# Down stage: gates fetched in quarters, first down weights one step earlier, lookup splits on DVE, sums by tile

## The reference, cut to what matters

```python
def chunk(xc):
    q = (xc @ w_q).reshape(PEER_CHUNK, PEER_HEADS, 2, PEER_DK_HALF)
    ...
    top_s, top_pos = lax.top_k(cand, PEER_TOPK)
    ids = jnp.take_along_axis(cand_id, top_pos, axis=-1)
    g = jax.nn.softmax(top_s, axis=-1)
    act = jnp.einsum('thkd,td->thk', u[ids], xc)
    w = g * jax.nn.gelu(act, approximate=False)
    return jnp.einsum('thk,thkd->td', w, v[ids])
...
h = h + peer_ffn(rms_norm(h, norm2_g[l]), ...)
```

## Time and profile before

| what | us |
|---|---|
| median of 3 runs | 3421.99 (3420.83 to 3426.84) |
| the profiled execution's own time | 3419.38 |
| its span | 3417.6 |
| PE busy | 3315.4 (97%) |
| DVE busy | 2617.1 (77%) |
| ACT busy | 1554.5 (45%) |
| POOL busy | 1110.6 (32%) |
| mean granted TensorE clock | 0.991 |

### The profile page before, as it was taken

How to read it: one execution, slowest core, us unless ns; L and a number is a source line. 1 busy time by engine, 2 the same in 40 slices (tenths; PEclk the granted TensorE clock), 3 DMA queues, 4 the chain that set the end, 5 groups by cost and what they waited for, 6 DMA issues and landing times.

```text
span 3417.6 us, 55668 instructions
## 1 busy us (share of the span) xinstructions
PE 3315.4 (97%) x19734; PEld 3073.7 (90%) x19734; DVE 2617.1 (77%) x4984; ACT 1554.5 (45%) x2366; POOL 1110.6 (32%) x717
## 2 busy tenths in 40 slices
PE   8999999999999899999999999999999998999998
PEld 7767878999999899999987678889999998999998
DVE  5555439999987788888755544499999877888887
ACT  5554333367773333333345443334677633333333
POOL 0000013433335355545200000143433354555552
PEclk9999999999999999999999999999999999999999
DMA  4113322589999999999621133225899999999996
GB/s 152 63 49 112 136 105 74 186 305 378 381 380 406 398 363 388 390 375 398 262 89 60 50 124 145 93 98 184 320 379 383 381 400 386 376 385 389 368 390 240
DMA packets 231895, 900.59 MB, mean 264 GB/s; under 512 B 21696, under 2 KB 66896, under 8 KB 183872
## 3 DMA queue, kind: packets, MB, share of 16 engines
q1 hardware_dynamic: 116752, 468.22, 36.5%
q0 software_dynamic: 93008, 337.91, 25.6%
q10 hardware_dynamic: 21984, 92.63, 6.8%
HBM read 804.31 MB, written 94.37 MB: 263 GB/s over the span
## 4 chain that ended last, share of the span: by engine, by line
PE 79%; DMA 8%; DVE 6%; ACT 3%; issue 3%; ACTq 0%; SPq 0%; DVEq 0%
PE bank L1282 23%; PE bank L1284 23%; PE bank L1283 23%; DMA raw<-in_stream 8%; PE bank L1580 5%; ACT hi L496 2%; DVE lo L808 2%; PE bank L1397 1%; PE bank L1412 1%; PE bank L1431 1%; PE bank L1530 1%; DVE rows L1118 1%; DVE act_in L1225 1%; DVE h L1179 0%; DVE w_lo L1230 0%
## 5 line engine op out<-in xcount | busy, mean ns | idle before, releaser
L808 DVE TENSOR_TENSOR lo<-raw,hi 128x2048 fp32r<-128x2048 f32 (+1 forms) x320 | 729.0, 2278 | 377.1 <-ACT hi L496 370.4
L1282 PE MATMUL bank<-xT_hi,hi 128*128 128x352 f32 (+1 forms) x2688 | 930.2, 346 | 12.7 <-DVE lo L808 10.8
L1284 PE MATMUL bank<-xT_hi,lo 128*128 128x352 f32 (+1 forms) x2688 | 914.1, 340 | 0.0
L1283 PE MATMUL bank<-xT_lo,hi 128*128 128x352 f32 (+1 forms) x2688 | 913.2, 340 | 0.0
L496 ACT ACTIVATE hi<-raw 128x2048 fp32r<-128x2048 f32 (+1 forms) x340 | 647.5, 1904 | 478.4 <-PE bank L1284 295.6
L1282 PE MATMUL bank<-w_hi,hi 128*128 128x352 f32 x2048 | 674.6, 329 | 32.8 <-DVE w_lo L1230 32.6
L1284 PE MATMUL bank<-w_hi,lo 128*128 128x352 f32 x2048 | 670.7, 327 | 0.0
L1283 PE MATMUL bank<-w_lo,hi 128*128 128x352 f32 x2048 | 665.1, 325 | 0.0
L1282 PEld LDWEIGHTS bank<-xT_hi,hi 128*128 128x128 f32 x2688 | 509.4, 189 | 47.0 <-issue 19.6
L485 POOL DMA_INDIRECT rows<-in_v_rows,ids x256 | 427.0, 1668 | 369.4 <-DVE h L1179 297.5
L1284 PEld LDWEIGHTS bank<-xT_hi,lo 128*128 128x128 f32 x2688 | 506.9, 189 | 26.2
(11 more groups left out here) (217 smaller groups left out, 4368.3 us busy)
## 6 DMA issues: line engine op xcount, KB each, us to landing
raw<-in_stream SPq DMA_DIRECT2D x352, 1024.0 KB
act_d<-act_s ACTq DMA_DIRECT2D x128, 352.0 KB
gate_d<-gate_s ACTq DMA_DIRECT2D x22, 2048.0 KB
act_in<-act_d SPq DMA_DIRECT2D x128, 352.0 KB
gate_in<-gate_d SPq DMA_DIRECT2D x28, 1408.0 KB
gate_in<-gate_d SPq DMA_DIRECT2D x12, 384.0 KB
rows<-in_u_rows,ids POOLq DMA_INDIRECT x256
rows<-in_v_rows,ids POOLq DMA_INDIRECT x256
```

What stands on the lines that cost most here:

```text
L808: dve.tensor_tensor(lo[s][:, 0:n], raw[s][:, 0:n], hi[s][:, 0:n].bitcast(F32), ALU.subtract).then_inc(lo_done, 1)
L1282: pe.matmul(dst, a_[0], b_[0], start=first, stop=False)
L1283: pe.matmul(dst, a_[0], b_[1], start=False, stop=False)
L1284: return pe.matmul(dst, a_[1], b_[0], start=False, stop=last)
```

## The change

Five things are done. (1) The gates of every load come in four parts of 2, 3, 3 and 3 slices of 11, one after each chunk of the load before, each part behind that chunk's `act_in`. The first load's parts stand ahead of every other of the 8 raw chunks in the tail, the second load's are issued over down chunks 0 to 3. (2) In the lookup POOL no longer splits chunks 9 and 14; DVE makes chunks 9 to 13 after a = 3, 5, 8, 10 and 13, and chunk 14 after the loop. (3) The first down weights (`weigh_step(0)`, `weights_hi(0, 0)`, `weigh_lo(0)`) are made in the up stage's last step, between that step's work. (4) ACT's gelu of the gathered rows' sums comes after two pairs of the down stage, its use on DVE (`weigh_rows`) at c = 6. (5) At the layer's end PE turns the sums back tile by tile, the spread only before the last; DVE scales tile 3 first, adds all three tiles, then scales them; of the next layer's transposes only banks 0 and 1 are written before all adds are done.

```diff
-X_BANKS = ((0, 1, 2, 3), (4, 5), (6, 7), ()), ((0, 1, 2, 3, 4), (5,), (6,), (7,))
+X_BANKS = ((0, 1), (2, 3, 4, 5, 6, 7), (), ()), ((0, 1, 2, 3, 4), (5,), (6,), (7,))
...
+ROW_PAIR = 2
...
-HALVED = range(2, 10)
-LOW_HALF_AT = (4, 7, 10, 12)
+HALVED = range(2, 9)
+LOW_HALF_AT = (3, 5, 8, 10, 13)
...
-                def load_gates(v, slot):
+                def load_gates(v, slot, part):
...
-                    sp.wait_ge(prod_done, done + V_CHUNKS * v - V_CHUNKS)
-                    sp.dma_start(gate_in[:, slot].rearrange("p q i t -> p q (i t)"),
-                                 gate_d[:, :, cols].rearrange("q j f -> j q f")).then_inc(gate_ld[slot], 16)
...
+                    if not (isinstance(v, int) and v < 2):
+                        sp.wait_ge(prod_done, done + V_CHUNKS * v - V_CHUNKS)
+                    sp.dma_start(gate_in[:, slot, q].rearrange("p q i t -> p q (i t)"),
+                                 gate_d[q, :, cols].rearrange("q j f -> j q f")).then_inc(gate_ld[slot], 16)
...
-                        if c == 1 and not last:
-                            load_gates(v + 1, 1 - slot)
+                        if not last:
+                            load_gates(v + 1, 1 - slot, c)
...
                 for j in range(2 * GATE_PARTS):
-                    first_gates(j // GATE_PARTS, j % GATE_PARTS)
+                    if j % 2 == 0:
+                        load_gates(0, 0, j // 2)
                     load_raw(lp + P_V - 5 + j // 2, j % 2)
...
+                    load_gates(1, 1, c)
                 v_loads(1, 1)
...
-                wait_alone(pool, lo_done, 2 * (lp + P_U + J_G) + CR, pool_passed)
-                split_lo(lp + P_U + J_G, 0)
...
+                def tail_steps(j, last_pair=False):
                     for s in range(2):
                         ahead(lp + P_U + j, s)
+                        if last_pair and s == 1:
+                            weights_hi(0, 0)
                         gelu(j, s, 0)
                         gelu(j, s, 1)
                         store_act(j, s)
-                weights_hi(0, 0)
...
                     if a in LOW_HALF_AT:
                         next_chunk = low_half()
-                assert next_chunk == FIND_STEPS
+                next_chunk = low_half()
+                assert next_chunk == FIND_STEPS + 1
...
+                    if st == C_U - FIND_STEPS - 1:
+                        weigh_step(0)
+                        row_op(n)
+                        n += 1
+                        weigh_lo(0)
...
-                weigh_step(0)
-                weigh_lo(0)
                 assert n == U_ROW_OPS
                 for c in range(C_V - 1):
                     ahead(lp + P_V + c // 2, c % 2)
                     weigh_step(c + 1)
-                    if c == 2:
+                    if c == 2 * ROW_PAIR + 2:
                         weigh_rows()
...
+                row_scale(2 * l + 2, 0)
                 for tt in range(NDT):
                     dve.wait_ge(y_ps, NDT * l + tt + 1)
...
                     last.then_inc(h_done, 1)
-                    row_scale(2 * l + 2, tt)
-                row_scale(2 * l + 2, NDT)
+                for i in range(1, NT):
+                    row_scale(2 * l + 2, i)
...
-                    if half == 0 and i < NDT:
-                        pe.wait_ge(h_done, NT * q + i + 2)
+                    if half == 0 and i == 1:
+                        pe.wait_ge(h_done, NT * q + NT)
...
+                pe.wait_ge(yT_act, NK // 2 * (l + 1) - 1)
+                pe.wait_ge(yT_dve, NK // 2 * (l + 1) - 1)
                 for tt in range(NDT):
-                    for d in V_BLOCKS[NK - 2:]:
+                    if tt == NDT - 1:
+                        pe.wait_ge(row_done, ROW_OPS * l + U_ROW_OPS + E)
+                        for nh in range(2):
+                            pe.matmul(ps[2 * NDT + nh][:], spread[:], y_e[:, nh * T:(nh + 1) * T], start=True, stop=True)
+                    for x, d in enumerate(V_BLOCKS):
+                        if tt == 0 and x == NK - 2:
+                            pe.wait_ge(yT_act, NK // 2 * (l + 1))
+                            pe.wait_ge(yT_dve, NK // 2 * (l + 1))
                         last = turn_back(d, tt)
                     last.then_inc(y_ps, 1)
```

More of the change, by code:

```diff
@@ L773, in weights_hi @@
                     act.activation(w_hi[:, s], act_in[:, s], ACT.Copy).then_inc(w_hi_done, 1)
-                with act.Fori(J_TAIL, C_U // 2) as j:
+                def tail_steps(j, last_pair=False):
                     for s in range(2):
                         ahead(lp + P_U + j, s)
+                        if last_pair and s == 1:
+                            weights_hi(0, 0)
                         gelu(j, s, 0)
@@ L780, in _ @@
                         store_act(j, s)
-                weights_hi(0, 0)
-                act.wait_ge(row_done, ROW_OPS * l + U_ROW_OPS)
-                act.activation(w_row[:], act_row[:], ACT.Gelu).then_inc(row_gelu, 1)
+                with act.Fori(J_TAIL, C_U // 2 - 1) as j:
+                    tail_steps(j)
+                tail_steps(C_U // 2 - 1, True)
                 def v_steps(j, last_pair=False):
@@ L790, in v_steps @@
                             weights_hi(2 * j + s + 1, 1 - s)
-                with act.Fori(0, C_V // 2 - 1) as j:
+                with act.Fori(0, ROW_PAIR) as j:
+                    v_steps(j)
+                act.wait_ge(row_done, ROW_OPS * l + U_ROW_OPS)
+                act.activation(w_row[:], act_row[:], ACT.Gelu).then_inc(row_gelu, 1)
+                with act.Fori(ROW_PAIR, C_V // 2 - 1) as j:
                     v_steps(j)
@@ L1186, in weigh_rows, with weigh_step, weigh_lo @@
                     dve.wait_ge(row_weighed, l + 1)
-                dve.wait_ge(lo_done, 2 * (lp + P_U + J_G) + 1 + CR)
                 wait_alone(dve, idx_ev, NDT * (l + 1) + 1, dve_passed)
+                def weigh_step(c):
+                    s, k, v = c % 2, l * C_V + c, l * V_LOADS + c // V_CHUNKS
+                    dve.wait_ge(act_ld[s], 16 * (k // 2 + 1))
+                    dve.wait_ge(gate_ld[v % 2], 16 * GATE_PARTS * (v // 2 + 1))
+                    a_ = act_in[:, s].rearrange("p i (q t) -> p i q t", t=SLICE)
+                    i = 2 * (c % V_CHUNKS)
+                    g_in = gate_in[:, v % 2, :, i:i + 2].rearrange("p q i t -> p i q t")
+                    dve.tensor_tensor(a_, a_, g_in, ALU.mult).then_inc(prod_done, 1)
+                def weigh_lo(c):
+                    s, k = c % 2, l * C_V + c
+                    dve.wait_ge(w_hi_done, k + 1)
+                    dve.tensor_tensor(w_lo[:, s], act_in[:, s], w_hi[:, s].bitcast(F32), ALU.subtract).then_inc(w_done, 1)
                 n = 0
@@ L1215, in _ @@
                         n += 1
-                def weigh_step(c):
-                    s, k, v = c % 2, l * C_V + c, l * V_LOADS + c // V_CHUNKS
-                    dve.wait_ge(act_ld[s], 16 * (k // 2 + 1))
-                    dve.wait_ge(gate_ld[v % 2], 16 * (v // 2 + 1 + (GATE_PARTS - 1) * (l + 1)))
-                    a_ = act_in[:, s].rearrange("p i (q t) -> p i q t", t=SLICE)
-                    i = 2 * (c % V_CHUNKS)
-                    g_in = gate_in[:, v % 2, :, i:i + 2].rearrange("p q i t -> p i q t")
-                    dve.tensor_tensor(a_, a_, g_in, ALU.mult).then_inc(prod_done, 1)
-                def weigh_lo(c):
-                    s, k = c % 2, l * C_V + c
-                    dve.wait_ge(w_hi_done, k + 1)
-                    dve.tensor_tensor(w_lo[:, s], act_in[:, s], w_hi[:, s].bitcast(F32), ALU.subtract).then_inc(w_done, 1)
-                weigh_step(0)
-                weigh_lo(0)
                 assert n == U_ROW_OPS
@@ L1636, in _ @@
                 pe.sem_inc(w_used, 1)
-                pe.wait_ge(row_done, ROW_OPS * l + U_ROW_OPS + E)
-                pe.wait_ge(yT_act, NK // 2 * (l + 1) - 1)
-                pe.wait_ge(yT_dve, NK // 2 * (l + 1) - 1)
-                for nh in range(2):
-                    pe.matmul(ps[2 * NDT + nh][:], spread[:], y_e[:, nh * T:(nh + 1) * T], start=True, stop=True)
                 def turn_back(d, tt):
@@ L1647, in turn_back @@
                     return pe.transpose(ps[2 + 2 * tt + d // 4][0:n, tile(d % 4)], yT[:, d, tt * P:tt * P + n], ident[:])
-                for d in V_BLOCKS[:NK - 2]:
-                    for tt in range(NDT):
-                        turn_back(d, tt)
-                pe.wait_ge(yT_act, NK // 2 * (l + 1))
-                pe.wait_ge(yT_dve, NK // 2 * (l + 1))
-                for tt in range(NDT):
-                    for d in V_BLOCKS[NK - 2:]:
+                pe.wait_ge(yT_act, NK // 2 * (l + 1) - 1)
+                pe.wait_ge(yT_dve, NK // 2 * (l + 1) - 1)
+                for tt in range(NDT):
+                    if tt == NDT - 1:
[6 more added lines that the diff above has]
+                            pe.wait_ge(yT_dve, NK // 2 * (l + 1))
                         last = turn_back(d, tt)
```

4 lines of the change are left out of this document (removed).

## The result

| what | before | after |
|---|---|---|
| median, us | 3421.41 (3417.52 to 3426.84, 4 runs) | 3360.45 (3356.21 to 3361.25, 4 runs) |
| the profiled execution's own time | 3419.38 | 3359.76 |
| its span | 3417.6 | 3357.9 |
| mean granted clock | 0.991 | 0.997 |

A forecast was written before the change was run, and what follows sets the result against it. PE was taken as the bound, ending the chain for 79% of the span. 48 + 10 + 3.6 = 61.6 us off 3419.4 gave 3357.8, with the median 2.6 above: 3360 us; 8 in 10 from 3344 to 3388.

The forecast's parts named there:

- the largest part: Tails and down stages, by gates in quarters and earlier first down weights: 59.9 - 10 - 2 = 48 us gained.
- The last step: From the profiled execution's forecast 3357.8 us to the median of the runs, taken as 2.6 us above it: 3360 us.
- Where the loss was: 60 us lost in tails and down stages of both layers, where raw chunks stand behind gates in the queue.
- rival D: Down stages: gates do not delay raw, perhaps bursts of row gathers do; quarters change nothing, 25 us gained, 3397 us; 7%.
- The 10 us of what stays in steady state: Loss left in both layers after quartering the gates, from late chunks and SP's wait for the product: 10 us.
- none of the delay shows: Lower bound for raw chunks issued up to 1.3 us later behind SP's wait for the product; upper bound 36 us.
- The 2 us at the starts: Loss left at the down stages' starts after making the first down weights earlier: 1 us a layer.
- I leave 1 us a layer: Down stage's start: w_lo done about when the last up matmul is, leaving 1 us of the 5.0 us wait and 1.7 clock.
- Rival B: DMAs simply full: a steady mix gives 385 GB/s, 124 chunks lose 32 us instead of 10; 3382 or 3390 us; 20%.
- Rival C: Each of 84 added gate transfers costs x us; slower than before from x = 0.73, 3486 us at 1.5; 4%.
- Lookup: End of the up stage: moving two splits from POOL to DVE cuts PE's wait for indices, 5 us a layer, 10 us.
- End: Layer's end: sums and scalings begin earlier, 2.6 us at the very end and 1 us between the layers, 3.6 in all.

The follow-up runs named there:

- the kernel with gates alone: The kernel before with only the gates fetched in four parts, one after each chunk: 3375.22 us, ratio 0.9854.
- the lump put back: The changed kernel with each load's four gate parts back to back again from load 2 on: 3389.74 us, ratio 0.9902 against the kernel before.
- the kernel with 104 blocks: The changed kernel with 104 gathered u blocks worked off in the gate steps instead of 96, so 56 instead of 64 in the tail: 3345.62 us.
- 112 blocks: The changed kernel with 112 gathered u blocks worked off in the gate steps instead of 96, 48 in the tail: 3342.29 us.
- the four at once: The kernel before with each load's gates, from the second load on, in four transfers back to back after the second chunk: 3406.55 us, ratio 0.9953.

## Why the prediction was right

The forecast was 3360, the measurement 3360.45. The mechanisms that were to bring the gain are confirmed one by one above. That the numbers meet within 0.5 us is luck: the steps were less exact than their sum, and two terms of the largest part were off in opposite directions, 10 us of late chunks in the steady stage where there were none, and 2 us at the starts where there were 15. The last step was off as well: the profiled execution was forecast at 3357.8 and took 3359.76, and its median lay 0.7 us above it, not 2.6.

*Where the loss was* held. The down stages take 509 and 507 us as forecast (505 to 510); no issue of a raw chunk in them takes over 0.47 us, where nine took over 1 us before; PE's wait for w_lo, 12.1 us, just misses "under 12". 60 us over pace in tails and down stages; some 15 are left (13.4 in the first down chunks, 1.7 in one tail chunk of 9.34 us), against 12 forecast. The gates did delay raw: rival D is refuted by the kernel with gates alone and, from the other side, by the lump put back.

*The 10 us of what stays in steady state* was misplaced. No chunk after the fifth is late. SP's first part of a load did wait for the product, and raw behind it, as the prediction said:

```profile
1190.21 0.38 SPq L383 DMA_DIRECT2D gate_in<-gate_d  x1
1190.64 0.47 SPq L367 DMA_DIRECT2D raw<-in_stream  x1
```

DVE had ended lo at 1189.38 and the product at 1190.18. This raw chunk is one of the late ones, split after a wait of 2.02 us, so here the delay may have cost a little. In the steady stage it cost nothing visible: the 150 us window has PE at 150.00, and the kernel with 104 blocks loses nothing at this place either. The bound of "none of the delay shows" was the right end.

*The 2 us at the starts* were too few. The gap ahead of the first down matmul is 0.4 us in the first layer, from 5.0, and the clock stays at 1.00 over it (1.3 us in the second layer). But the first five chunks lose 6.5 and 7 us over 7.84 each. The step that failed is "I leave 1 us a layer": it costed the first product and its waits on DVE, and neither a transfer nor the row work ahead of the second chunk. After the wait went, two things came next. The first chunk (9.55 us) was held by DVE: three pieces of row work, two of them after idle times of 0.5 and 0.6 us, stood ahead of the second chunk's lo, and its w_lo began only at 1173.80. With 104 blocks two pieces stand there without idle time, and the chunk takes 7.88. From the third chunk on raw was late. ACT's timeline over the first layer's chunks 3 and 4 shows it:

```profile
1185.14 1.92 ACT L491 ACTIVATE hi<-raw 128x2048 fp32r<-128x2048 f32 x1 [4.02 <-DMA raw<-in_stream]
...
1195.68 1.92 ACT L491 ACTIVATE hi<-raw 128x2048 fp32r<-128x2048 f32 x1 [4.59 <-DMA raw<-in_stream]
```

The prediction had the sign of this in its own rows, 413 and 411 GB/s at a share of 1.03 in the tails' ends, and read it as a rate that is good to have. It was close to the most that was seen: no window of 93 us shows over 415 in any kernel here. The kernel with 104 blocks showed that what it meant in the tail was a queue behind. The rate alone does not say so, as the 416 GB/s with 112 blocks show; the sign that goes with it is DVE's waits for u rows, 16.7 us in the first layer's tail from 1067 us on.

*Rival B*, DMAs simply full, is refuted for the steady stage (398 GB/s moved with PE never idle) and true from the end of the tail into the first down chunks. *Rival C*, a price for each transfer, fell with the four at once: x is not above zero. The Trainium skill ("DMA: Bandwidth & Descriptors", Bandwidth) has the rule that DMAs be batched to at least 1 MiB. The runs of this case do not agree with it for these gates: in parts of 256 and 384 KB beside raw chunks of 1 MB the DMAs moved 398 GB/s, and four such parts in the place of 1408 KB were faster. The 2 us that the prediction set for x stand on the same page of the Trainium skill (Anatomy of one DMA) for a DMA that GpSimd issues, and mostly as the time until completion is reported; the gates are issued by SP.

*Lookup*: 10 forecast. Chunks 13 and 14 went from 22.7 to 17.4 us and from 23.7 to 17.5, 11.5 in all. DVE's timeline there, answering to the earlier trace rows:

```profile
691.27 0.69 DVE L1116 TENSOR_SCALAR rows<-rows 128x1024 f32<-128x1024 f32 x1
691.88 2.80 DVE L1119 COPY_PREDICATED rows<-rows,top_i 128x1024 uint32<-128x1024 uint32 x2
694.57 2.28 DVE L809 TENSOR_TENSOR lo<-raw,hi 128x2048 fp32r<-128x2048 f32 x1
696.76 0.69 DVE L1127 TENSOR_REDUCE g_sum<-g_t 128x32 f32<-128x512 f32 x1
```

Two copies take 2.80 us instead of 6.99, as costed.

*End*: 3.6 forecast, 2.5 at the very end (14.2 to 11.7 us from the last down matmul to the end of the last scaling) and 1.6 between the layers (590.0 to 588.4 us from the last down matmul to the second up stage; up to the first product of the second layer it is 15.7 to 13.7). The sign to look for was wrong, though: the first sum comes 0.8 us earlier after the last matmul, not 3. DVE's timeline at the end:

```profile
3345.80 1.28 DVE L851 SCALAR_TENSOR_TENSOR xs<-h,rstd,raw 128x1024 f32<-128x1024 f32 x1
3347.00 3.67 DVE L1266 TENSOR_TENSOR h<-h,bank 128x512 f32<-128x512 f32 x6
...
3353.56 1.28 DVE L851 SCALAR_TENSOR_TENSOR xs<-h,rstd,raw 128x1024 f32<-128x1024 f32 x1
```

The scaling of tile 3 fills the first 1.3 us, and then six sums run without a gap where they were three pairs. The work was the same and began earlier, so the price held.

*Two slips of the prediction's arithmetic* change nothing. 3049 KB a chunk are 2.98 MiB, not 3.05; the 3.12 MB and the 398 GB/s are right. And with nothing left of the 60 us and the lookup at 12 the lower end of its range comes to 3346 or 3347, not 3344.

## What to carry to other kernels

In a queue that is worked off in order, a large transfer that isn't urgent should be cut and its parts put between the urgent ones; here that was worth 49 us by itself, of the 61 of the whole change, and cutting without spreading only 16. When DMAs run near the highest rate of the whole kernel and an engine waits for their data, read it as a queue that is behind and ask where the debt is paid: here it was one stage later, and moving 8 blocks of 512 KB a layer out of the full stretch was worth another 15 us. Parts that are measured one by one add up only where they don't free the same stretch.

## What the runs showed of the hardware

The most that the core's DMAs moved here is 415 GB/s over 93 us, at a share of 1.03, and 416 over 50 us, at 1.02. The first of these was the tail of the kernel after, with DVE waiting for rows; in the second, and in the tail with 104 blocks at 401 GB/s and 1.02, nothing waited for a DMA. One transfer of 1408 KB delayed what came behind it more than four of 256 to 384 KB with the same bytes (16 us over the kernel, give or take 8); I had expected no difference, and its cause is open. An issue of a raw chunk on SP mostly takes 0.33 us, and up to 3.6 us behind such gates, one or four; behind spread parts none in the down stages took over 0.47. A comparison of 128 x 1024 on DVE took 0.70 us alone and 2.73 beside POOL's subtraction, a predicated copy 1.37 and 3.58.
